# A decoder layer on one Trainium2 core: a norm handed from VectorE to ScalarE and GpSimd, and half of a one-hot gather written as products of halves

## The reference

```
x = x + hier_moe(rms_norm(x, ffn_norm_g), ...)
    p_coarse = softmax(ht @ w_coarse + b_coarse);  grp = argmax(p_coarse)
    fine = (ht @ w_fine + b_fine)[the 4 experts of grp];  top 2 of softmax(fine)
    for e in range(16):
        he = silu(ht @ w_gate[e]) * (ht @ w_up[e])
        y = y + combine[:, e:e+1] * (he @ w_down[e])
```

## Time and profile before

| | |
|---|---|
| median of 3 runs | 787.72 us (787.14 to 789.12) |
| the profiled execution | 787.38 us |
| its span in the trace | 785.5 us, 1.9 us less than its time |
| mean granted TensorE clock | 0.988 of full |
| busy share of the span | PE 96%, DVE 68%, ACT 58%, POOL 23% |
| PE's longest idle stretch here | 5.0 us, in front of the rank products at 465.35 us |

### The profile page before, as it was taken

The page is one execution under the profiler, slowest core; times in us unless marked ns, Lnnn a source line. Parts: engine busy times, 40 slices in busy tenths (PEclk is TensorE's granted clock), DMA queues, the critical chain, the costliest instruction groups (busy, mean ns, idle before and its releaser), DMA issues.

```text
span 785.5 us, 11565 instructions
## 1 busy us (share of the span) xinstructions
PE 751.7 (96%) x4124; PEld 582.1 (74%) x4124; DVE 537.3 (68%) x711; ACT 456.9 (58%) x665; POOL 179.9 (23%) x185
## 2 busy tenths in 40 slices
PE   4999999999999999999999969999999999999994
PEld 3978789777788889888788844677777777777763
DVE  5445378598782455622555488599989889899986
ACT  4455662487883236433443242587887887787862
POOL 3800023000001011000000100135555444555312
PEclk9999999999999999999999989999999999999997
DMA  9934521000405435542104768999999999999942
GB/s 297 233 94 141 155 83 59 1 2 2 161 3 188 134 108 177 172 151 66 53 1 143 310 236 321 398 380 381 383 370 373 382 372 375 380 384 384 385 154 107
DMA packets 61902, 166.88 MB, mean 212 GB/s; under 512 B 8224, under 2 KB 36192, under 8 KB 49576
## 3 DMA queue, kind: packets, MB, share of 16 engines
q1 hardware_dynamic: 56376, 150.69, 51.8%
q0 software_dynamic: 4480, 12.48, 6.8%
q10 hardware_dynamic: 1008, 3.21, 1.2%
HBM read 153.44 MB, written 12.85 MB: 212 GB/s over the span
## 4 chain that ended last, share of the span: by engine, by line
PE 93%; DVE 3%; DMA 1%; ACT 1%; issue 1%; POOL 0%; SPq 0%; POOLq 0%; ACTq 0%; DVEq 0%
PE ps L1976 24%; PE ps L1978 23%; PE ps L1977 23%; PE ps L2249 3%; PE ps L2197 3%; PE ps L2175 2%; PE ps L2444 2%; PE ps L2287 2%; PE ps L2178 1%; PE ps L2108 1%; PE ps L2424 1%; PE ps L2366 1%; DMA raw<-in_w_in 1%; PE ps L2179 1%; PE ps L2430 1%
## 5 line engine op out<-in xcount | busy, mean ns | idle before, releaser
L1356 DVE TENSOR_TENSOR wlo<-raw,whi 128x2048 fp32r<-128x2048 f32 x29 | 66.5, 2292 | 78.5 <-ACT whi L878 78.4
L1976 PE MATMUL ps<-whi,mhi 128*96 128x512 f32 (+1 forms) x276 | 110.1, 399 | 2.0 <-DVE mlo L1909 1.2
L1978 PE MATMUL ps<-whi,mlo 128*96 128x512 f32 (+1 forms) x276 | 109.3, 396 | 0.0
L1977 PE MATMUL ps<-wlo,mhi 128*96 128x512 f32 (+1 forms) x276 | 108.8, 394 | 0.0
L1371 DVE TENSOR_TENSOR wlo<-arena,whi 128x2048 fp32r<-128x2048 f32 x39 | 89.4, 2291 | 20.4 <-ACT whi L897 20.4
L741 POOL TENSOR_SCALAR stat<-stat 128x1 f32<-128x1 f32 x18 | 11.3, 630 | 355.9 <-ACT tok L903 209.4
L897 ACT ACTIVATE whi<-arena 128x2048 fp32r<-128x2048 f32 x39 | 74.7, 1915 | 26.4 <-PE ps L1978 26.4
L878 ACT ACTIVATE whi<-raw 128x2048 fp32r<-128x2048 f32 x29 | 55.4, 1910 | 48.5 <-PE ps L1978 48.4
L1976 PE MATMUL ps<-ahi,whi 128*128 128x512 f32 x192 | 75.6, 394 | 0.0
L1978 PE MATMUL ps<-ahi,wlo 128*128 128x512 f32 x192 | 74.8, 390 | 0.0
L1977 PE MATMUL ps<-alo,whi 128*128 128x512 f32 x192 | 74.8, 390 | 0.0
(11 more groups left out here) (396 smaller groups left out, 1692.4 us busy)
## 6 DMA issues: line engine op xcount, KB each, us to landing
arena<-in_exp_w_gate SPq DMA_DIRECT2D x30, 1024.0 KB, 14.4
arena<-in_exp_w_up SPq DMA_DIRECT2D x17, 1024.0 KB, 14.2
raw_a<-in_exp_w_down SPq DMA_DIRECT2D x16, 1024.0 KB, 15.2
raw<-in_exp_w_up SPq DMA_DIRECT2D x15, 1024.0 KB, 13.3
arena<-in_exp_w_down SPq DMA_DIRECT2D x9, 1024.0 KB, 18.6
raw<-in_exp_w_down SPq DMA_DIRECT2D x7, 1024.0 KB, 15.1
raw<-in_w_in SPq DMA_DIRECT2D x5, 1024.0 KB, 7.3
raw<-in_w_in SPq DMA_DIRECT2D x10, 512.0 KB, 5.6
```

The costliest lines, as they stand in the source:

```text
L1356: v.tensor_tensor(wlo[:, n % SPLIT, :], raw[:, n % RAW, :], whi[:, n % SPLIT, :].bitcast(F32), ALU.subtract).then_inc(lo_done, 1)
L1976: mm(out_, ahi_, bhi_, start=first, stop=False)
L1977: mm(out_, ahi_, blo_, start=False, stop=False)
L1978: return mm(out_, alo_, bhi_, start=False, stop=last)
```

## The change

ACT makes `X[3]` times the reciprocal root into `tok[:, 2, :]`, and POOL multiplies that by the gain into `H3[3]`; DVE's `norm_last(3)` goes. ACT rounds `H3[0]` and `H3[1]` into `mhi`, POOL subtracts that from them into `mlo`. The four picks of tiles 0 and 1 each become two products with fp32r operands (high, then low), with the one-hot matrices of those tiles held in an fp32r tile; the picks of tiles 2 and 3 stay plain. ACT does its three new copies ahead of `split_expert(4)`; POOL does its three ahead of its wait for the lists. Bank 0's tiles are taken in the order 0, 2, 1, 3.

```diff
-        first_hot = work[:, 2096:2096 + NT * CHUNK].rearrange("p (t s) -> p t s", t=NT)
+        hot_r = wrt2[:, :, :].rearrange("p k n -> p (k n)")[:, 0:2 * CHUNK].rearrange("p (t s) -> p t s", t=2)
+        hot_f = work[:, 2096:2096 + NT * CHUNK].rearrange("p (t s) -> p t s", t=NT)
+        first_hot = [hot_r[:, t, :] if t < 2 else hot_f[:, t, :] for t in range(NT)]
...
+            pool.wait_ge(gain_full, 64)
+            pool.wait_ge(h_done, N4 - 1)
+            pool.wait_ge(pick_act, 1)
+            lanes = "t (q k) -> t q k"
+            pool.tensor_tensor(H3[:, NT - 1, :].rearrange("t (k q) -> t q k", k=KD), tok[:, 2, :].rearrange(lanes, k=KD),
+                               gbc[:, :].rearrange(lanes, k=KD), ALU.mult).then_inc(h_done, 1)
+
+            for t in range(2):
+                pool.wait_ge(pick_act, t + 2)
+                pool.tensor_tensor(mlo[:, D * t:D * (t + 1)], H3[:, t, :], mhi[:, D * t:D * (t + 1)].bitcast(F32), ALU.subtract)\
+                    .then_inc(pick_lo, 1)
...
+            act.wait_ge(rms_done, N4)
+            a.activation(tok[:, 2, :], X[:, NT - 1, :], ACT.Copy, scale=stat[:, 2, N4 - 1:N4]).then_inc(pick_act, 1)
+            for t in range(2):
+                act.wait_ge(h_done, N3 + t + 1)
+                a.activation(mhi[:, D * t:D * (t + 1)], H3[:, t, :], ACT.Copy).then_inc(pick_act, 1)
             split_expert(4)
...
             for t in range(NT):
-                v.tensor_scalar(first_hot[:, t, :], siota, rank[:, t, 0:1], R[:, 636 + t:637 + t],
+                v.tensor_scalar(first_hot[t], siota, rank[:, t, 0:1], R[:, 636 + t:637 + t],
                                 ALU.is_equal, ALU.mult).then_inc(first_done, 1)
             v.tensor_copy(cnt, ps[2][:, 0:NEXP]).then_inc(first_done, 1)
-            norm_last(3)
...
             def pick(t, b):
-                return mm(ps[4 + b][0:CHUNK, :], first_hot[:, t, :], H3[:, t, 512 * b:512 * b + 512],
-                          start=(t == 0), stop=(t == NT - 1))
+                out_, c = ps[4 + b][0:CHUNK, :], slice(D * t + 512 * b, D * t + 512 * b + 512)
+                if t < 2:
+                    mm(out_, first_hot[t], mhi[:, c], start=(t == 0), stop=False)
+                    pe.wait_ge(pick_lo, t + 1)
+                    return mm(out_, first_hot[t], mlo[:, c], start=False, stop=False)
+                return mm(out_, first_hot[t], H3[:, t, 512 * b:512 * b + 512], start=False, stop=(t == NT - 1))
...
-            for t in range(NT):
+            pe.wait_ge(pick_act, 3)
+            for t in (0, 2, 1, 3):
                 pe.wait_ge(first_done, t + 1)
                 if t == NT - 1:
                     pe.wait_ge(h_done, N4)
```

More of the change, by code:

```diff
@@ L489, in build @@
         h_done = sem("h_done")
+        pick_act = sem("pick_act")
+        pick_lo = sem("pick_lo")
         ntp_done = sem("ntp_done")
```

## The result

The changed kernel takes 790.3 us (median of 9 runs, 789.75 to 791.64) against 787.45 us for the kernel before in the same comparison (9 runs, 785.28 to 789.12). The ratio is 1.0038, with a 95% interval of 1.0026 to 1.0051: slower by about 0.4%. The interval leaves out 1, but the difference is small, and executions of one and the same kernel lie up to 4 us apart. The profiled execution took 790.14 us with a span of 788.3 us, 2.8 us more than before.

What follows compares the result with a forecast made beforehand. DVE's routing chain was taken as the path from 460.4 to 466.7 us, then PE. Profiled 787.4 plus 7.2 (chain held by POOL) minus 1.6 (picks) gave 793.0 us, range 788.3 to 795.6.

Steps and rivals of the forecast that it cites:

- step 1: In DVE's routing chain from 461.15 us, links held until POOL's products end; stall 7.2 us, PE's idle about 12 us.
- the allowance of 0.4 for the permuted write: POOL's first product, writing permuted columns, was taken at 2.7 us where a plain one was taken at 2.3.
- gaps of 0.1 between products: Between POOL's three products, gaps of 0.1 us, bringing their sum of 7.3 us to 7.5.
- Rival C: DVE's routing chain keeps POOL out; POOL then delays the one-hot matrices and lists, 3.6 us late: 791.0 us, chance 0.19.
- Rival B: POOL and DVE do not exclude each other in the routing chain; DVE on time, 785.8 us or 784.9, chance 0.15.
- step 3: PE's picks: four of eight become pairs with 0.43 or 0.23 us between starts, 1.6 us less in all.
- The 2.5 us of a clock that rises with the work: At PE's picks, the saving if the clock rose later by the same work instead of the same time.
- a fixed time, as the forecast took it: Clock rise after PE's restart at the picks comes as long after it as before, adding nothing to the difference.
- step 4: DVE without its 1.97 us norm: lists ready some 0.8 us ahead of PE, worth nothing by itself.
- ACT's copies: ACT's three copies ahead of its weight splits cost nothing, or 0.2 us if the exponentials are late.
- step 5: After 498 us, the same rows as before, all moved by one amount.

Runs made afterwards that it cites:

- add_memsets: The kernel before with three idle POOL memsets of 128 x 2048 added where the change has its POOL products: 788.01 us, ratio 1.0003.
- add_copies: The kernel before with three idle POOL copies of 128 x 1024, one SBUF input each, added at the place of the change's products: 789.0 us, ratio 1.0010.
- norm_part_pad: norm_part with a tiny DVE memset and its wait in the place of the norm taken out: 790.45 us, ratio 1.0035.
- norm_part: The kernel before with only the norm of tile 3 moved from DVE to ACT and POOL, picks left plain: 788.94 us, ratio 1.0016.
- picks_part: The kernel before with only the halves and paired picks of tiles 0 and 1, the norm left on DVE: 791.3 us, ratio 1.0030.
- padded changed kernel: The changed kernel with a tiny DVE memset and its wait in the place of the norm taken out: 790.97 us, ratio 1.0032.
- early_lists_late_pad: early_lists_late with a tiny DVE memset and its wait added: 785.19 us, ratio 0.9957 to the kernel before.
- before_pad: The kernel before with a tiny DVE memset and its wait added, no work taken away: 785.34 us, ratio 0.9962.
- early_lists_late: The kernel before with tiles 0 and 1 picked as halves made earlier, and the lists' product behind half of the second expert piece: 784.28 us, ratio 0.9957.

## Why the prediction was right, and where it was off

The forecast was 793.0 us, 5.6 more than the profiled execution before; measured were 790.3, 2.9 more than the median before. The direction and the mechanism came out as forecast, the size at about half.

- **The chain is held** (step 1). Right in mechanism: the links end where POOL's products end. The stall was 6.2 us, not 7.2. POOL's product takes 2.37 us with permuted columns and 2.33 without; the 2.3 was right and the allowance of 0.4 for the permuted write was wrong, and the gaps of 0.1 between products did not exist. The three products took 6.98 us (460.99 to 467.97), and in that time the chain did four links that take 0.83 us before, one held link at the end of each product and a reduction; the prediction had given it little more than the reduction.
- **The skill's rule.** The Trainium skill, "SBUF — State Buffer", section "Who interferes with whom", says that a DVE instruction with two SBUF inputs contends with a GpSimd instruction that reads SBUF and not with one that only writes it. add_memsets and add_copies agree on both halves (0.17 us and 0.72 us for the same link), and norm_part_pad, norm_part and the change agree with a lock for the whole instruction (2.37 us for the link beside a product of 2.37). The section words the full block for DVE's two-port modes and speaks of an exclusive lock in general; the prediction put the two together, and the runs bear it out. The Trainium skill, "GPSIMD Engine Reference", section 3.1, gave an estimate of 2.25 us per product, half of its figure for an addition of 2048 columns; the trace has 2.33 to 2.37. By the page's price the stall would have been 6.8, nearer than mine.
- **Rival C**, POOL kept out by the chain, did not happen: POOL's first product started at 460.99, between a reduction and the next link, and the other two each started where the one before ended. **Rival B** is refuted.
- **The picks** (step 3). 1.41 us instead of 1.6. Four picks changed as told, but the low clock lasted longer, from the restart at 471.42 to 476.9, which is 5.5 us against 5.0 before; at half speed that is the missing 0.2. The 2.5 us of a clock that rises with the work did not come, and the same work does not give the same rise: before and norm_part do the same picks, with low stretches of 5.0 and 6.7 us behind the restart. But neither is it a fixed time, as the forecast took it: over the thirteen profiles it was 4.2 to 7.3 us. That the two profiles compared here lie within 0.5 us is in part luck; the term had an uncertainty of about 1 us that the range did not name.
- **DVE without the norm** (step 4). Right: worth nothing by itself (norm_part), and picks_part shows the wait of 0.99 us that it keeps away.
- **ACT's copies**. Right: no wait of PE or DVE goes back to them.
- **After 498 us all moved by one amount** (step 5). This is the step that failed. It took the stretch between the lists and the first full turn as rigid. Between the lists and 502 us the changed kernel's profile came without a low-clock stretch that had cost 1.56 us and with a gap shorter by 0.35 us. With the two terms the sum is 787.4 + 6.1 - 1.4 - 1.9 = 790.2; without them it would have been 792.1, within 0.9 of the 793.0 forecast. The experiments show that the gap follows what DVE's program holds. Why it takes one of two values was not found, nor why the stretch stayed out of the padded changed kernel's profile even with the long gap.
- Without those 1.9 us the change costs about 4.7 us in its own terms (6.1 - 1.4), and what the halves are worth with the POOL reads moved out of the chain is small: early_lists_late_pad and before_pad, both without the low stretch in their profiles and in the same comparison, took 785.19 and 785.34. Their runs overlap (783.88 to 785.63 and 784.91 to 786.31), so the 1.0 us expected of the halves is neither shown nor excluded. early_lists_late beats both kernels of this study by median. Against the five executions of the kernel before in its comparison that had a mean clock of 0.991 (785.15 to 785.38) its 784.28 is 1.0 us less, so some 2.3 of its 3.3 us are probably the low stretch that it lacks.

## What to carry to other kernels

Before giving idle POOL a wide instruction that reads SBUF, look at what DVE does in that stretch: a chain of short two-input links is a bad neighbour, because a product stops the chain for about its whole length (2.2 us for one of 2.37 here). Put it beside DVE work that reads PSUM, as early_lists_late does at 452 us, or beside DVE's idle time, and mind that DVE's two-input instruction holds a small POOL step in the same way. When a kernel's time moves by 0.2 to 0.4%, compare the granted clock stretch by stretch before crediting the edit, and try the kernel with one idle instruction added: here that moved the median by 3.2 us, more than the change did.

## What the runs showed of the hardware

- A POOL product of two 128 x 1024 tiles takes 2.33 to 2.37 us, with the same time for a write in permuted columns, for which DVE pays 2069 against 1280 ns. A POOL copy of that size with rounding takes 1.04 to 1.08 us, a memset of twice the size 1.85 us (5.54 us for three).
- When both engines had work ready, one DVE link ended at the end of each POOL product, and the next product began at once. In the loop over the experts, where DVE's subtractions follow each other without a wait, POOL's copy of 96 x 1 lasted through two of them (4.74 us at the median in the earlier trace rows, against subtractions of 2.29 us).
- A tiny DVE instruction added about 25 us earlier moved the start of a later DVE instruction by 0.37 us against PE in three kernels of four, and in the kernel before the granted clock from 494 to 498 us went from 0.57 to 1.00 with it. The kernel before itself shows executions near 785.3 and others from 787 to 789.
- After PE's idle stretch of 5 to 11 us the low clock lasted 4.2 to 7.3 us behind the restart, and 5.0 and 6.7 us with the same work behind it.
